# Mixers' last borders: weight halves split sooner, filler spread over steps, two kinds of work given to GpSimd, head loads issued ahead of weight units

## The reference

```
layer 0:  x += 0.5*gate * swiglu(mod(norm(x)))           # ffn0
          x += gate * (moba_attention(q, k, v) @ w_o)     # mixA, woA
          x += 0.5*gate * swiglu(...)                     # ffn1
          kv bands for 3 dilated branches from x          # kv
layer 1:  ffn2;  x += gate * (dilated_attention @ w_o)    # mixB, woB
          ffn3;  final norm
qkv = h @ w_qkv;  q, k = rope(q), rope(k)
p = softmax(mask(q @ k.T / 8));  o = p @ v;  y = concat_heads(o) @ w_o
```

## Time and profile before

| | us |
|---|---|
| median of 3 runs | 2383.8 (2383.27 to 2386.54) |
| the profiled execution, by the same clock | 2387.28 |
| its span in the trace | 2385.5 |
| PE busy in the span | 2341.2 |
| DVE, ACT, POOL busy | 1320.3, 876.0, 274.0 |
| granted TensorE clock, mean | 0.993 |

### The profile page before, as it was taken

The page is one execution under the profiler, slowest core; times in us unless marked ns, Lnnn a source line. Parts: engine busy times, 40 slices in busy tenths (PEclk is TensorE's granted clock), DMA queues, the critical chain, the costliest instruction groups (busy, mean ns, idle before and its releaser), DMA issues. The chain is left out here.

```text
span 2385.5 us, 31355 instructions
## 1 busy us (share of the span) xinstructions
PE 2341.2 (98%) x11245; PEld 1941.6 (81%) x11245; DVE 1320.3 (55%) x2090; ACT 876.0 (37%) x1397; POOL 274.0 (11%) x367
## 2 busy tenths in 40 slices
PE   9999999999899999999999999999999989999998
PEld 6888888788778888888888888888888877888886
DVE  7555544776575554455554555544767766333333
ACT  3322223456543332233332333322456654333321
POOL 0000000334200000004222000000133521000000
PEclk9999999999999999999999999999999999999999
DMA  6666543576446564437777766543678872333332
GB/s 251 193 193 192 174 132 96 205 250 238 138 149 187 184 197 133 124 93 251 237 234 258 251 186 187 166 138 102 222 265 303 310 239 76 104 94 99 94 94 87
DMA packets 128896, 424.90 MB, mean 178 GB/s; under 512 B 14112, under 2 KB 22944, under 8 KB 128288
## 3 DMA queue, kind: packets, MB, share of 16 engines
q1 hardware_dynamic: 111392, 356.55, 46.7%
q0 software_dynamic: 17408, 67.12, 8.1%
HBM read 352.84 MB, written 69.21 MB: 177 GB/s over the span
## 5 line engine op out<-in xcount | busy, mean ns | idle before, releaser
L405 DVE TENSOR_TENSOR w_lo<-w_raw,w_hi 128x1024 fp32r<-128x1024 f32 (+1 forms) x386 | 472.0, 1223 | 599.7 <-ACT w_hi L401 599.4
L410 PE MATMUL ps<-h_hi,w_hi 128*128 128x512 f32 x1872 | 744.2, 398 | 11.6 <-DVE w_lo L405 9.3
L412 PE MATMUL ps<-h_hi,w_lo 128*128 128x512 f32 x1872 | 733.7, 392 | 0.0
L411 PE MATMUL ps<-h_lo,w_hi 128*128 128x512 f32 x1872 | 733.5, 392 | 0.0
L401 ACT CAST w_hi<-w_raw 128x1024 fp32r<-128x1024 f32 (+2 forms) x388 | 395.8, 1020 | 745.5 <-PE ps L412 733.6
L410 PEld LDWEIGHTS ps<-h_hi,w_hi 128*128 128x128 f32 x1872 | 354.3, 189 | 88.1 <-DVE w_lo L405 13.2
L412 PEld LDWEIGHTS ps<-h_hi,w_lo 128*128 128x128 f32 x1872 | 354.2, 189 | 76.0
L411 PEld LDWEIGHTS ps<-h_lo,w_hi 128*128 128x128 f32 x1872 | 354.4, 189 | 68.8 <-issue 0.2
L410 PE MATMUL ps<-act_hi,w_hi 128*128 128x512 f32 x704 | 275.3, 391 | 0.0
L412 PE MATMUL ps<-act_hi,w_lo 128*128 128x512 f32 x704 | 274.0, 389 | 0.0
L411 PE MATMUL ps<-act_lo,w_hi 128*128 128x512 f32 x704 | 273.9, 389 | 0.0
(11 more groups left out here) (206 smaller groups left out, 2770.1 us busy)
## 6 DMA issues: line engine op xcount, KB each, us to landing
w_raw<-gate_up SPq DMA_DIRECT2D x176, 512.0 KB, 3.7
ada_raw<-ada SPq DMA_DIRECT2D x144, 512.0 KB, 4.6
w_raw<-down SPq DMA_DIRECT2D x80, 512.0 KB, 3.6
w_raw<-kv_w SPq DMA_DIRECT2D x48, 512.0 KB, 3.7
w_raw<-mixa_w SPq DMA_DIRECT2D x34, 512.0 KB, 3.8
w_raw<-mixb_w SPq DMA_DIRECT2D x34, 512.0 KB, 4.5
kb<-rot_st POOLq DMA_DIRECT2D x24, 512.0 KB, 4.8
kb<-att POOLq DMA_DIRECT2D x24, 512.0 KB, 5.3
```

Of the source, the lines that this page charges most:

```text
L405: eng.tensor_tensor(w_lo[:, slot, 0:n], w_raw[:, slot, 0:n], w_hi[:, slot, 0:n].bitcast(F32), ALU.subtract).then_inc(w_lo_done[slot], 2)
L410: nc.tensor.matmul(out_ap, l_hi, r_hi, start=start, stop=False, skip_group_check=skip)
L411: nc.tensor.matmul(out_ap, l_hi, r_lo, start=False, stop=False, skip_group_check=skip)
L412: return nc.tensor.matmul(out_ap, l_lo, r_hi, start=False, stop=stop, skip_group_check=skip)
```

## The change

Five things move; no arithmetic is added or dropped.

1. The filler of the last borders. Part 2b comes one step later (in step 0, not ahead of it). Tile 3's parts go from steps 2 and 3 to 1 and 2 in A, and from 2 and 5 to 4 and 8 in B.
2. The weight halves of units 2 and 3 of the output projection. ScalarE casts unit 2 ahead of the last `collect` of the group instead of behind it, and unit 3 right behind that group (A) or in step 0 ahead of `collect` (B). VectorE subtracts unit 3 right behind unit 2 (A) or at the end of step 0 (B), and in A it subtracts the unit of step 15 ahead of `collect`. In B the unit of step 15 is subtracted ahead of `rot_low`.
3. GpSimd takes row 5's low half (steps 4 and 9) and the low halves of output units 5 and 7 from VectorE.
4. In mixer A, GpSimd's two rope halves go from one step to two (2 and 3, 7 and 8), and VectorE's low half of unit 6 of a group from step 10 to 11.
5. SyncE issues loads of heads ahead of weight units: q of head 0 in A ahead of unit 8, head 15 of A ahead of output units 6 and 7, head 2 of a group in B ahead of unit 6, head 14 of B ahead of output units 4 and 5.

```diff
-SPLIT_LO = {1: 3, 3: 4, 6: 5, 10: 6, 15: 7}
+SPLIT_LO = {"A": {1: 3, 3: 4, 6: 5, 11: 6, 15: 7}, "B": {1: 3, 3: 4, 6: 5, 10: 6, 15: 7}}
 OUT_SUBSTEPS = {
-    "A": out_table({-1: "2a 2b", 2: "3a", 3: "3b", 6: "2c", 7: "3c", ...
+    "A": out_table({-1: "2a", 0: "2b", 1: "3a", 2: "3b", 6: "2c", 7: "3c", ...
-    "B": out_table({-1: "2a 2b", 2: "3a", 5: "3b", 10: "2c", 11: "3c", ...
+    "B": out_table({-1: "2a", 0: "2b", 4: "3a", 8: "3b", 10: "2c", 11: "3c", ...
-OUT_LOW = {layer: {step + 1: n for step, n in high.items() if n < 9} ...
+OUT_LOW = {layer: {step + 1: n for step, n in high.items() if n in (4, 6, 8)} ...
+OUT_LOW["B"][0] = 3
+POOL_LOW = {layer: {step + 1: n for step, n in high.items() if n in (5, 7)} ...
-POOL_ROWS = (0, 1, 2, 3, 4, 6)
-POOL_IN = {"A": {13: 6}, "B": {2: 4, 17: 6}}
+POOL_ROWS = (0, 1, 2, 3, 4, 5, 6)
+POOL_IN = {"A": {4: 5, 13: 6}, "B": {2: 4, 9: 5, 17: 6}}
...
@@ rope_add: one half or both
-            nc.gpsimd.tensor_tensor(*operands(0), ALU.subtract).then_inc(rope_done, 1)
-            if halves == 1:
+            if 0 in halves:
+                pool.wait_ge(rot_lo_done, n)
+                nc.gpsimd.tensor_tensor(*operands(0), ALU.subtract).then_inc(rope_done, 1)
+            if 1 not in halves:
                 return
...
@@ sp_mixer, group_a (g = 0), group_b, and the last group
+                    if a is None and j == 2:
+                        load_q(sp, "A", g, 0)
                     unit(g, 6 + j)
...
-                unit(g, 6)
                 for j in (2, 3):
                     load_k(sp, "B", a, j)
                     load_q(sp, "B", a, j)
+                    if j == 2:
+                        unit(g, 6)
...
                 load_v(sp, "A", a, 2)
+                loads(3)
                 out_unit(30)
                 out_unit(31)
-                loads(3)
...
+            loads(2)
             out_unit(28)
             out_unit(29)
-            loads(2)
...
@@ act_mixer
+                    if s == STEPS - 1 and not early:
+                        act_out_high(act, "wo" + layer, 2)
                     collect(a * STEPS + s)
                 if early:
                     split(8)
-                else:
-                    act_out_high(act, "wo" + layer, 2)
+                elif is_a:
+                    act_out_high(act, "woA", 3)
...
+                if s == 0 and not is_a:
+                    act_out_high(act, wo, 3)
@@ dve_mixer
+                    last_a = is_a and not early and s == 15
+                    begin(a * STEPS + s, (lambda: split(SPLIT_LO[layer][15])) if last_a else None)
+                    if s in SPLIT_LO[layer] and not last_a:
+                        split(SPLIT_LO[layer][s])
...
                     dve_out_low(dve, "wo" + layer, 2)
+                    if is_a:
+                        dve_out_low(dve, "woA", 3)
...
-                if s in OUT_IN[layer] and OUT_IN[layer][s] == OUT_BY_POOL:
-                    dve_out_in(dve, wo, OUT_BY_POOL)
@@ pool_mixer
-            adds = {2: 0, 7: 1} if is_a else {1: 0, 7: 1, 14: 2}
+            adds = {2: (0, (0,)), 3: (0, (1,)), 7: (1, (0,)), 8: (1, (1,))} if is_a else \
+                {1: (0, (0, 1)), 7: (1, (0, 1)), 14: (2, (0,))}
...
+                if s in POOL_LOW[layer]:
+                    n = POOL_LOW[layer][s]
+                    w_split_lo(pool, UNIT0[wo] + n, 1, out_width(n))
```

More of the change, by code:

```diff
@@ L143 @@
 OUT_SUBSTEPS = {
-    "A": out_table({-1: "2a 2b", 2: "3a", 3: "3b", 6: "2c", 7: "3c", 8: "4a", 9: "4b", 10: "4c", 11: "5a",
+    "A": out_table({-1: "2a", 0: "2b", 1: "3a", 2: "3b", 6: "2c", 7: "3c", 8: "4a", 9: "4b", 10: "4c", 11: "5a",
                     12: "5b", 13: "5c", 14: "6a", 15: "6b", 16: "6c 0x", 17: "7a 7b", 18: "7c 1x"}),
-    "B": out_table({-1: "2a 2b", 2: "3a", 5: "3b", 10: "2c", 11: "3c", 12: "4a", 13: "4b", 14: "4c", 15: "5a",
+    "B": out_table({-1: "2a", 0: "2b", 4: "3a", 8: "3b", 10: "2c", 11: "3c", 12: "4a", 13: "4b", 14: "4c", 15: "5a",
                     16: "5b 5c", 17: "6a", 18: "6b", 19: "6c", 20: "0x 7a", 21: "7b 7c", 22: "1x"})}
-OUT_HIGH = {"A": {0: 3, 6: 4, 7: 5, 10: 6, 13: 7, 16: 8, 18: 9},
-            "B": {0: 3, 10: 4, 11: 5, 14: 6, 16: 7, 20: 8, 22: 9}}
-OUT_LOW = {layer: {step + 1: n for step, n in high.items() if n < 9} for layer, high in OUT_HIGH.items()}
+OUT_HIGH = {"A": {6: 4, 7: 5, 10: 6, 13: 7, 16: 8, 18: 9},
+            "B": {10: 4, 11: 5, 14: 6, 16: 7, 20: 8, 22: 9}}
+OUT_LOW = {layer: {step + 1: n for step, n in high.items() if n in (4, 6, 8)} for layer, high in OUT_HIGH.items()}
+OUT_LOW["B"][0] = 3
+POOL_LOW = {layer: {step + 1: n for step, n in high.items() if n in (5, 7)} for layer, high in OUT_HIGH.items()}
 OUT_ADD = {"A": {0: 0, 1: 1, 7: 2, 8: 3, 11: 4, 14: 5, 17: 6, 19: 7}, "B": {1: 0, 2: 1, 11: 2, 12: 3, 15: 4, 17: 5, 21: 6, 23: 7}}
 OUT_IN = {"A": {4: 5, 12: 6}, "B": {0: 4, 8: 5, 16: 6}}
-POOL_ROWS = (0, 1, 2, 3, 4, 6)
-POOL_IN = {"A": {13: 6}, "B": {2: 4, 17: 6}}
+POOL_ROWS = (0, 1, 2, 3, 4, 5, 6)
+POOL_IN = {"A": {4: 5, 13: 6}, "B": {2: 4, 9: 5, 17: 6}}
 POOL_IN_AHEAD = {"mixA": {11: (0,), 12: (1,), 13: (2,), 14: (3,), 15: (4,)}, "mixB": {11: (0,), 12: (1,), 13: (2,), 14: (3,)}}
-OUT_BY_POOL = 5
+OUT_BY_POOL = 6
 OUT_IN_AHEAD = {"mixA": {10: (0,), 11: (1,), 12: (2,), 13: (3,), 14: (4,)}, "mixB": {10: (0,), 11: (1,), 12: (2,), 13: (3,)}}
@@ L674, in pe_out_part @@
                     pe.wait_ge(out_in_low, (0 if name == "woA" else len(POOL_ROWS)) + k + 1)
-                elif tile == 2 and k == OUT_BY_POOL:
-                    pe.wait_ge(h_lo_done, h_count(name) + k + 1)
                 cols = slice((k + at) * P, (k + at + 1) * P)
@@ L1532, in rope_multiply, with rope_add @@
                 op.then_inc(pair_free, 1)
-        def rope_add(pool, pair, n, late=None, half_n=None, chunks=False, halves=2):
+        def rope_add(pool, pair, n, late=None, half_n=None, chunks=False, halves=(0, 1)):
             def operands(half):
@@ L1854, in group_a @@
                         load_v(sp, "A", a, j + 1)
+                    if a is None and j == 2:
+                        load_q(sp, "A", g, 0)
                     unit(g, 6 + j)
                 load_k(sp, "A", g, 0)
-                load_q(sp, "A", g, 0)
+                if a is not None:
+                    load_q(sp, "A", g, 0)
                 unit(g, 9)
@@ L2099, in dve_out_in @@
                                     classes(h_hi[:, k, :].bitcast(F32)),
-                                    ALU.subtract).then_inc(h_lo_done, k + 1 if k == OUT_BY_POOL else 2)
+                                    ALU.subtract).then_inc(h_lo_done, KT)
         def dve_out_low(dve, name, n):
@@ L2224, in fold_add, with begin @@
                 nc.vector.tensor_tensor(to, *of, ALU.add).then_inc(att_done[layer], 1)
-            def begin(st):
+            def begin(st, ahead=None):
                 joins = not is_a and st % 4 == 1 and 5 <= st <= ROWS + 1
@@ L2237, in begin @@
                     invert(st - 1)
+                if ahead is not None:
+                    ahead()
                 collect(st - 1)
@@ L2359, in begin, with add @@
                     scale(st - 5)
-            def add(g, pair):
+            def add(g, pair, halves=(0, 1)):
                 n = g * (2 if is_a else 3) + rope0 // 2 + pair
@@ L2365, in add @@
                          (1 if is_a else 1 + pair) if pair > 0 and first else None, chunks=not is_a and pair == 0,
-                         halves=1 if not is_a and pair == 2 and g > 0 else 2)
+                         halves=(0,) if not is_a and pair == 2 and g > 0 else halves)
             def store(g, pair):
@@ L2404, in pool_mixer @@
                     if s in adds:
-                        add(g, adds[s])
+                        add(g, *adds[s])
                     if s in stores:
```

4 lines of the change are left out of this document (removed).

## The result

The changed kernel takes 2373.4 us (median of 6 runs, 2371.0 to 2374.9), the kernel before, beside it, 2383.7 (2383.3 to 2389.5). The ratio is 0.9949 with a 95% interval of 0.9937 to 0.9961: faster by 9 to 15 us. The forecast was 2363.6, a gain of 20.2; its first rival stood at 2375. About half of the forecast gain came: 10.3 us between the medians, 12 by the ratio. The profiled executions are 14.0 us apart (spans 2385.5 and 2371.5), so most of what follows is read from stretches of the trace and not from whole times.

The account below looks back on a forecast made before the run. PE, busy 98%, bounds the kernel, so only its idle time and low-clock losses could be won back. Six terms in the mixers summed to 20.2 us: 2383.8 - 20.2 = 2363.6 us, own range 2358 to 2370, 8 in 10 2357 to 2376.

Parts of the forecast that it names:

- first rival: New waits take half of the last borders' gain: A's border 4, B's -3, unit 8 late; 2375 us, chance 0.26.
- GpSimd's halves: Middle groups of A: splitting the rope adds lets the first scaling end sooner and removes waits for `probs`; 2.2 us.
- head 15: Head 15 of A: its k, issued ahead of two weight units, lands sooner and the wait for `k_lo` goes; 1.9 us.
- head 2 of B: Loads issued 2.4 us sooner without unit 6 in front; the wait of 2.17 and its low clock go; 3.3 us.
- Last border of A: Three causes of waiting go, of 10.5 us lost; less 1.6 new idle and 1.0 for half a low-clock spell: 7.9 us.
- (b): Last border of A: unit 3's cast no longer stands behind an exponential, so PE can start tile 3 sooner; not sized separately.
- (c): Last border of A: row 5's `h_lo` no longer holds VectorE and the next maximum, where PE waited 1.48 us.
- part (a): Last border of A: step 15's low half, issued ahead of `collect`, is done sooner; PE's wait of 0.59 us goes.
- Head 0 of A: q issued 3.7 us sooner, ahead of unit 8; the wait for `q_st` and its low clock go; 3.4 of 4.9 us.
- Last border of B: Head 13's q bounds it: 2.3 won, 1.4 lost, 0.6 from small VectorE waits; 1.5 us, ends -3 and 8.
- The second (loads gain nothing): Bytes in the queues set landings, so heads 0, 15 and 2 give 0; 2372 us, chance 0.06.
- The rule against the change: Low halves moved to GpSimd hold up VectorE's two-input SBUF operations through a shared read interface; up to 1 us less gain.

Follow-up runs that it names:

- middle_old: The changed kernel with GpSimd's rope adds in one piece, head 15's k behind units 30 and 31, and head 2 of B behind unit 6: ratio 0.9984.
- b_filler_old: The changed kernel with the filler of B's last border at its old steps (2a 2b at -1, 3a at 2, 3b at 5): ratio 0.9940.
- a_unit3_late: The changed kernel with A's unit 3 split where it was before (cast behind step 0, low half in step 1): ratio 0.9953.
- a_row5_vector: The changed kernel with row 5's low half of A made by VectorE in step 4 again: ratio 0.9951.
- b_row5_first: The changed kernel with GpSimd making row 5's low half of B ahead of the scaling of step 9, not behind it: ratio 0.9934.
- b_two_fixes: The changed kernel with the edits of b_row5_first and b_filler_old together: ratio 0.9946.
- b_adds_ahead: b_three_fixes with B's first two residual adds (tiles 0 and 1) on VectorE ahead of step 0, not in steps 1 and 2: ratio 0.9935.
- b_three_fixes: b_two_fixes with unit 3's low half of B made by GpSimd in step 0 instead of VectorE: ratio 0.9949.

## Why the prediction was right and wrong

- **The size**: 2373.4 lies outside the forecast's own range (2358 to 2370) and inside that of 8 in 10 (2357 to 2376), which rivals 1 and 2 had widened. In the pair two of the six terms make 7.5 us of the miss, and the other four give 1.4 back.
- **What bounds the kernel**: right. Everything gained came from idle time and clock in the mixers; PE's idle outside them did not change (16.9 us before and 17.2 after, outside group 0 to head 15 of A and head 2 to head 15 of B).
- **GpSimd's halves, head 15, head 2 of B**: right in mechanism and size, shown by taking them back (8.4 us for a forecast of 7.4). Head 15's is the loosest: 2.2 in the pair, 1.1 against the second profile of before, 1.4 in middle_old. Head 2's is 3.5, 2.9 and 4.4.
- **Last border of A**: right, 8.3 for 7.9; in the ten profiles with the new border untouched it took 32.4 to 33.9 us, mean 33.0, against 40.7 and 40.6. The new waits came to 2.4 us, not 1.6, and the half spell (1.0) did not come: that the two misses cancel is luck. Seven of the ten have a fourth wait, of 0.35 to 1.45 us for unit 4's low half, which the sum does not have; it is longest where unit 4 landed latest (6.8 us after its issue in b_filler_old, 5.3 in after, where there is none). Parts (b) and (c) are shown by a_unit3_late and a_row5_vector; part (a) was not tried by itself.
- **Head 0 of A**: the failed step is "k and q should land before PE's filler ends", with 3.4 of the 4.9 taken. q landed 3.7 us after its issue; k has unit 8's 0.5 MB in front of it now: in b_row5_first `k_lo` took 6.75 us and TensorE waited 1.44 for it; after, it landed at 455.96, and the chance wait of 1.77 hid that. Then head 1's q came late in its turn. Of the 4.9 the 1.7 of clock went, and the idle time stayed (3.4 before, 4.0 after, 3.0 to 3.9 elsewhere with this order): it was spread over three waits. I had put the price on unit 8 alone and not followed the loads to head 1.
- **Last border of B**: the failed step is the sum "2.3 less 1.4, plus 0.6", a term of 1.5 that measured -3.0 in the pair and -0.4 between the means. Its idle time was near: 1.1 us less in the pair. The two prices named there were both real: the wait behind the scaling was 2.0 for a forecast of 1.4, and VectorE's low half in step 0 with empty steps 1 to 3 gave 1.16 and 1.57, which the sum carried at nothing (the first goes when GpSimd makes that half, the second when 3a stands in step 2). What the sum had wrong is clock: it stood nowhere in it, where the bound of -3 had a spell for each, and it is 8.8 us in the pair against 3.6, with 3.6 to 8.8 in the six. A's border had its half spell, B's had none.
- **The profiled execution**: "the gain is the same there" was wrong by up to 3.7 us (14.0 in the pair, 10.3 between the first medians, 12 by the ratio). Executions of the kernel before ran from 2380 to 2393 us. Of those beside b_two_fixes the fastest (2379.9) had a mean clock of 0.996 and the slowest (2389.2) 0.991: 0.005 x 2384 = 12 us of clock, more than the whole difference.
- **Rivals**: the time is nearer to the first (2375) than to the forecast, and two of its three prices were paid in the pair (B's border, head 0, the latter by k and head 1's q and not by unit 8). The third, A's border at 4, was not, so that the number is close to this rival is in part luck. Its "the low clock needs only waits of 2 us" does not hold as it stands: a wait of 2.71 us had none behind it, and one of 1.48 had. The second (loads gain nothing) held for head 0 alone.
- **The rule against the change** (beside GpSimd, VectorE's two-input operations are held up) I gave up to 1 us and no chance. In A's border it cost nothing to be seen: the low half of step 15 took 1.50 us beside GpSimd after and 1.77 before, and TensorE did not wait for it. At head 0, which the change doesn't touch in this respect, it decides by chance between a wait of 1.8 and none.

No version is shown to beat the changed kernel: b_row5_first (0.9934) and b_adds_ahead (0.9935) lie 3.6 and 3.3 us lower by the ratio, with intervals that overlap its 0.9937 to 0.9961. In the trace three fixes have the shortest last border of B, 57.1, in one profile. Open: whether head 13's q could come sooner, if heads 13's and 14's k and v stood behind its store; this was not tried.

## What to carry to other kernels

When several loads are wanted within a few microseconds, an order only chooses which is late: follow every load that an order moves, to the next head and not only to the one at hand. Clock is part of the price of each new wait, and as it comes and goes between executions with the same waits, a term from one pair of profiles is worth no more than its spread; cut the traces at the same instructions and compare several. Before work is moved ahead of a wait, look for the next chain that sets the same instruction: here a queue of 10 us in front of one small load gave back 3.6 us.

## What the hardware showed unexpectedly

- The same pair of operations, VectorE's low half (two operands in SBUF) and GpSimd's adds 0.65 us behind, ended in one of two ways: 1.21 and 1.71 us, or 4.29 and 1.31, with the same spacing. GpSimd was issuing a DMA (0.53 us) when the low half began, 0.42 us into it, in both.
- An operation of 8 columns on VectorE took 1.20 us (`weight`, 0.16 elsewhere) beside GpSimd's low half in b_three_fixes.
- The same waits can cost different clock. In B's last border the kernel before waited 2.18 and 2.94 us in both its profiles and lost 3.6 us of clock in one and 7.0 in the other; after and middle_old, both with the new border, lost 8.8 and 3.6. In A a single wait of 2.7 us (a_unit3_late) was followed by none, while one of 1.5 us (a_row5_vector), behind two of 0.9 and 1.0, was.
